# A two-block network on one core: five layer norms run in two halves of 256 tokens, and attention's prologue and branch phase are put in another order

## The reference

```
for l in range(DEPTH):          # DEPTH = 2
    x = layer_norm(alpha * x + 0.5 * swiglu_ffn(x, ffn1_wi[l], ffn1_wo[l]), ln_g[l, 0], ln_b[l, 0])
    mix = even_mixer(x, ...) if l % 2 == 0 else odd_mixer(x, ...)
    x = layer_norm(alpha * x + mix, ln_g[l, 1], ln_b[l, 1])
    x = layer_norm(alpha * x + 0.5 * swiglu_ffn(x, ffn2_wi[l], ffn2_wo[l]), ln_g[l, 2], ln_b[l, 2])
```

```
h = rms_norm(x, g_pre_mix[l]);  proj = h @ w_in[l]
gates = sigmoid(gate_pre.reshape(B, S, 3, D) + b_gate[l])
merged = gates[:, :, 0] * (o_a @ w_br_a[l]) + gates[:, :, 1] * (o_b @ w_br_b[l]) + gates[:, :, 2] * (o_m @ w_br_m[l])
x = x + rms_norm(merged @ w_out[l], g_post_mix[l])
```

## Time and profile before

| | |
|---|---|
| runs of the kernel before, us | 3979.09, 3987.4, 3988.2 (median 3987.4) |
| profiled execution, its own time | 3980.04 us |
| its span | 3978.3 us, mean TensorE clock 0.956 |
| TensorE busy | 3690.6 us, 93% |
| VectorE, ScalarE, GpSimd busy | 1725.9, 1354.3, 606.2 us |

### The profile page before, as it was taken

How to read it: one execution, slowest core, us unless ns; L and a number is a source line. 1 busy time by engine, 2 the same in 40 slices (tenths; PEclk the granted TensorE clock), 3 DMA queues, 4 the chain that set the end, 5 groups by cost and what they waited for, 6 DMA issues and landing times. The chain is left out here.

```text
span 3978.3 us, 44285 instructions
## 1 busy us (share of the span) xinstructions
PE 3690.6 (93%) x17510; PEld 2955.4 (74%) x17510; DVE 1725.9 (43%) x1970; ACT 1354.3 (34%) x1723; POOL 606.2 (15%) x473
## 2 busy tenths in 40 slices
PE   8999987999899989887899989998999898998998
PEld 6887764788688868565688867776888786877886
DVE  2224563322422244753422254555664444547642
ACT  3223432322322233322322242344443323445432
POOL 2102002211311030131311041003110210012110
PEclk9999998999999999877899999999999999999999
DMA  3222211222222222000122233222222233222222
GB/s 138 95 90 95 85 43 43 94 95 87 83 95 98 88 92 85 29 1 13 63 97 96 92 116 111 96 69 95 95 95 91 103 114 104 82 101 85 95 89 80
DMA packets 62080, 339.98 MB, mean 85 GB/s; under 512 B 7024, under 2 KB 11520, under 8 KB 32768
## 3 DMA queue, kind: packets, MB, share of 16 engines
q1 hardware_dynamic: 61952, 338.19, 23.9%
HBM read 331.87 MB, written 6.29 MB: 85 GB/s over the span
## 5 line engine op out<-in xcount | busy, mean ns | idle before, releaser
L355 PE MATMUL bank<-x_hi,w_hi 128*128 128x512 f32 x3488 | 1391.9, 399 | 158.9 <-POOL x_lo L429 77.4
L356 PE MATMUL bank<-x_lo,w_hi 128*128 128x512 f32 x3488 | 1376.5, 395 | 0.0
L357 PE MATMUL bank<-x_hi,w_lo 128*128 128x512 f32 x3488 | 1374.9, 394 | 0.0
L324 DVE TENSOR_TENSOR w_lo<-raw,w_hi 128x2048 fp32r<-128x2048 f32 (+2 forms) x326 | 689.9, 2117 | 970.0 <-ACT w_hi L319 968.6
L355 PEld LDWEIGHTS bank<-x_hi,w_hi 128*128 128x128 f32 x3488 | 666.9, 191 | 337.2 <-issue 145.4
L319 ACT ACTIVATE w_hi<-raw 128x2048 fp32r<-128x2048 f32 (+2 forms) x326 | 567.7, 1742 | 761.6 <-PE bank L357 750.5
L357 PEld LDWEIGHTS bank<-x_hi,w_lo 128*128 128x128 f32 x3488 | 666.2, 191 | 141.4
L356 PEld LDWEIGHTS bank<-x_lo,w_hi 128*128 128x128 f32 x3488 | 666.8, 191 | 137.1 <-issue 1.0
L355 PE MATMUL bank<-f_g_hi,w_hi 128*128 128x512 f32 x704 | 275.5, 391 | 0.0
L357 PE MATMUL bank<-f_g_hi,w_lo 128*128 128x512 f32 x704 | 273.9, 389 | 0.0
L356 PE MATMUL bank<-f_g_lo,w_hi 128*128 128x512 f32 x704 | 273.9, 389 | 0.0
(11 more groups left out here) (402 smaller groups left out, 3425.7 us busy)
## 6 DMA issues: line engine op xcount, KB each, us to landing
raw<-in_weights SPq DMA_DIRECT2D x222, 1024.0 KB, 4.8
raw<-in_weights SPq DMA_DIRECT2D x96, 704.0 KB, 4.0
raw<-in_weights SPq DMA_DIRECT2D x8, 768.0 KB, 4.2
x_kept<-X SPq DMA_DIRECT2D x2, 2048.0 KB, 11.8
X<-x_kept SPq DMA_DIRECT2D x2, 2048.0 KB, 9.6
work<-in_rpb SPq DMA_DIRECT2D x12, 256.0 KB, 5.1
stats<-in_rpb SPq DMA_DIRECT2D x12, 256.0 KB, 5.3
X<-in_x SPq DMA_DIRECT2D x8, 256.0 KB, 6.3
```

The costliest lines, as they stand in the source:

```text
L324: dve.tensor_tensor(w_lo[:, s, 0:size], raw[:, s, 0:size], w_hi[:, s, 0:size].bitcast(F32), ALU.subtract).then_inc(lo_ready.sem, 1)
L355: pe.matmul(out, w_hi[:, s, w], hi(k), start=first and n == 0, stop=False)
L356: pe.matmul(out, w_hi[:, s, w], lo(k), start=False, stop=False)
L357: mm = pe.matmul(out, w_lo[:, s, w], hi(k), start=False, stop=last and n == len(kts) - 1)
```

## The change

Of the six layer norms five (all but the last before attention) are split by tokens. At the end of a stage `last_tile` makes the last product for tokens 0 to 255 first, then for tokens 256 to 511 in two parts with the first half's sums between them; the second half's sums are made in the next stage. At its start `lead_vector`, `lead_scalar`, `lead_pool` go through the eight tiles of the first half and then through those of the second, with the split of the second weight chunk (`split`) in between, and `lead_tensor` takes both first chunks: chunk 0 and 1 for the first half, then chunk 0 and 1 for the second, so that a slot is freed only in the second half. The split of chunk 2 is placed behind this on ScalarE and VectorE. The blocks of the two stages are joined: the engines don't meet between them. The first stage of all, which has no norm, runs in halves too. In attention, `merge` makes its three products from PSUM one behind the other, GpSimd adds the first two, VectorE adds the third in `join(n - 1)`, behind `merge(n)`; TensorE waits for the products alone. ScalarE splits weights ahead of `round_(n)`. In the prologue the first bias goes ahead of the weights' rest, their rounding behind value tile 1 and not 4, and the second part of the first scores behind tile 6 and not 4. The core of the diff:

```diff
+        def lead_vector(dve, split):
...
+            for t in range(2):
+                for k in range(KT + 1):
+                    if k == 0:
+                        if t == 0:
+                            half_variance(dve, norm[0], 0)
+                        dve.wait_ge(half_rstd[norm[0].p].sem, half_rstd[norm[0].p].at(2 * t + 2))
+                    if k < KT:
+                        scale(t, k)
+                    if k == 0:
+                        half_mean(dve, norm[0], t)
+                    if k:
+                        shift(t, k - 1)
+                    if t == 0 and k == 2:
+                        centre_half(dve, norm[0], 1)
+                    if t == 0 and k == 5:
+                        half_variance(dve, norm[0], 1)
+                if t == 0:
+                    split()
...
+        def lead_scalar(act, split):
+            if norm[0] is not None:
+                half_square(act, norm[0], 0)
+                half_scale(act, norm[0], 0)
+            for t in range(2):
+                for k in range(KT):
+                    x, q = X[:, k, halves[t]], t * KT + k
...
+                        act.wait_ge(lead_shifted.sem, lead_shifted.at(q + 1))
+                        act.activation(x, x, ACT.Identity, bias=col("ln_b", n), scale=col("ln_g", n)).then_inc(x_ready.sem, 1)
+                        act.wait_ge(x_ready.sem, x_ready.at(q + 1))
+                    act.activation(x_hi[:, k, halves[t]], x, ACT.Copy).then_inc(rounded.sem, 1)
+                    if t == 0 and k == (KT - 1 if norm[0] is None else 2):
+                        split()
+                    if t == 0 and norm[0] is not None:
+                        if k == 1:
+                            square_half(act, norm[0], 1)
+                        elif k == 4:
+                            half_square(act, norm[0], 1)
+                        elif k == 6:
+                            half_scale(act, norm[0], 1)
...
+        def lead_tensor(pe, n0):
+            pe.wait_ge(lo_ready.sem, PRIME + n0 + 1)
+            for t in range(2):
+                xt, yt = (lambda k: x_hi[:, k, halves[t]]), (lambda k: x_lo[:, k, halves[t]])
+                for k in range(KT):
+                    pe.wait_ge(split_ready.sem, split_ready.at(t * KT + k + 1))
+                    for v in range(2):
+                        mm = linear(pe, bank[v][:, halves[t]], n0 % 2, (v * KT + k) * P, [k], xt, yt, first=k == 0,
+                                    last=k == KT - 1, group=False)
+                    if t == 0 and k == 1 and norm[0] is not None:
+                        half_sums(pe, norm[0], 1)
+                        half_stats(pe, norm[0], 1)
+                if t == 1:
+                    mm.then_inc(chunk_used.sem, 1)
                 else:
+                    pe.wait_ge(lo_ready.sem, PRIME + n0 + 2)
+                for v in range(2):
+                    mm = linear(pe, bank[2 + v][:, halves[t]], (n0 + 1) % 2, v * KT * P, range(KT), xt, yt, group=False)
+            mm.then_inc(chunk_used.sem, 1)
...
+        def half_sums(pe, nb, t):
+            b = bank[7 - t]
+            if t:
+                pe.wait_ge(half_centred[nb.p].sem, half_centred[nb.p].at(2))
+            else:
+                pe.wait_ge(part_ready.sem, part_ready.at(KT - 2))
+                pe.wait_ge(square_used.sem, square_used.at(KT - 2))
+            pe.matmul(b[:, 0:HS], const["mean_d"], nb.acc[:, halves[t]], start=True, stop=False, skip_group_check=True)
+            pe.matmul(b[:, HS:S], const["mean_d"], nb.accq[:, halves[t]], start=False, stop=False, skip_group_check=True)
...
+        def last_tile(pe, nb, pieces, hi, lo):
+            for n, (c, at, ks) in enumerate(pieces):
+                first, last = n == 0, n == len(pieces) - 1
+                mm = linear(pe, out[0], c % 2, at, ks, part(hi, 0), part(lo, 0), first=first, last=last, group=False)
+                if first:
+                    pe.wait_ge(z_ready.sem, z_ready.at(KT - 1))
+                if not last:
+                    linear(pe, out[1], c % 2, at, ks, part(hi, 1), part(lo, 1), first=first, last=last, group=False)\
+                        .then_inc(chunk_used.sem, 1)
+                    continue
+                mm.then_inc(half_psum[nb.p].sem, 1)
+                half_sums(pe, nb, 0)
+                linear(pe, out[1], c % 2, at, ks[:4], part(hi, 1), part(lo, 1), first=first, last=False, group=False)
+                half_stats(pe, nb, 0)
+                linear(pe, out[1], c % 2, at + 4 * P, ks[4:], part(hi, 1), part(lo, 1), first=False, last=True, group=False)\
+                    .then_inc(chunk_used.sem, 1)
...
+                    sp.wait_ge(lead_shifted.sem, lead_shifted.at(KT))
...
-                    split(0, 0)
-                    lead_scalar(act)
+                    lead_scalar(act, lambda: split(0, 0))
+                    split(0, 1)
                     for j in range(n):
-                        if j:
+                        if j > 1:
                             split(j // 2, j % 2)
...
-                    lead_vector(dve)
+                    lead_vector(dve, lambda: split(0, 0))
+                    split(0, 1)
                     for j in range(n):
-                        split(j // 2, j % 2)
+                        if j > 1:
+                            split(j // 2, j % 2)
                         if j < GATES:
                             causal_conv(j, U, 2 * j, "rg_conv", 4, u_ready)
                         if j == 1:
...
-                            elif n == 4:
+                            elif n == 6:
                                 scores(0, 1)
...
@@ -2672,7 +2882,7 @@
                         for n in range(NT):
                             bank_copy(n)
-                            if n == 4:
+                            if n == 1:
                                 at_chunk(split_hi, act, g0 + 1)
                         exps(0)
                         for c in chunks_ending(-1):
...
                         for n in range(KT):
                             if n + 3 < KT:
                                 open_gates(n + 3)
-                            round_(n)
                             if n % 2:
...
                             gate = G[3 * n:3 * n + 3]
-                            ch.add(dve.tensor_tensor(m, b[0], gate[0], ALU.mult))
-                            ch.add(dve.tensor_tensor(q, b[1], gate[1], ALU.mult))
-                            ch.wait()
-                            ch.add(dve.tensor_tensor(m, m, q, ALU.add))
-                            ch.wait()
-                            ch.add(dve.tensor_tensor(q, b[2], gate[2], ALU.mult))
-                            ch.wait()
-                            dve.tensor_tensor(m, m, q, ALU.add).then_inc(y_ready.sem, 1)
+                            dve.tensor_tensor(m, b[0], gate[0], ALU.mult)
+                            dve.tensor_tensor(q, b[1], gate[1], ALU.mult).then_inc(pair_ready.sem, 1)
+                            dve.tensor_tensor(r, b[2], gate[2], ALU.mult).then_inc(state_ready.sem, 1)
+                        def join(n):
+                            v = n % 2
+                            dve.wait_ge(state_ready.sem, state_ready.at(n + 1))
+                            dve.wait_ge(h_ready.sem, h_ready.at(n + 1))
+                            dve.tensor_tensor(mg[:, v, :], mg[:, v, :], rest[:, v, :], ALU.add).then_inc(y_ready.sem, 1)
...
+                        add_bias(0)
                         at_chunk(split_lo, dve, g0 + 1)
-                        add_bias(0)
                         add_bias(0, 1)
...
+                        for n in range(KT + 1):
+                            if n < KT:
+                                merge(n)
+                            if n:
+                                join(n - 1)
                             if n % 2:
                                 at_chunk(split_lo, dve, b0 + n // 2 + 2)
...
                     def _(pool):
-                        for n in range(KT):
-                            pool.wait_ge(rounded.sem, rounded.at(n + 1))
-                            pool.tensor_tensor(x_lo[:, n, :], mg[:, n % 2, :], x_hi[:, n, :].bitcast(F32),
-                                               ALU.subtract).then_inc(split_ready.sem, 1)
+                        for n in range(KT + 1):
+                            if n < KT:
+                                m = mg[:, n % 2, :]
+                                pool.wait_ge(pair_ready.sem, pair_ready.at(n + 1))
+                                pool.tensor_tensor(m, m, part[:, n % 2, :], ALU.add).then_inc(h_ready.sem, 1)
+                            if n:
+                                pool.wait_ge(rounded.sem, rounded.at(n))
+                                pool.tensor_tensor(x_lo[:, n - 1, :], mg[:, (n - 1) % 2, :], x_hi[:, n - 1, :].bitcast(F32),
+                                                   ALU.subtract).then_inc(split_ready.sem, 1)
```

(13 more changed lines are left out.)

241 lines of the change are left out of this document (162 added, 79 removed).

## The result

The changed kernel took 3996.66 us (median of 12 runs, 3991.78 to 4000.83); the kernel before, timed beside it, 3985.01 us (12 runs, 3972.15 to 3998.6). The ratio is 1.0028, with a 95% interval of 1.0016 to 1.0039: slower, by about as little as this kernel's runs can tell. The forecast was 3979, slightly faster. The time lies in the range (3951 to 4004), the direction was wrong. The 3985.01 is a median of runs that lie up to 26 us apart; the kernel before that was timed beside the experiments has medians of 3979.9 to 3980.2.

The account below looks back on a forecast made before the run. TensorE, busy 93% of the span, was taken as the bound, with only waits and slow stretches to win. Seams +12.2, prologue +11.4, branch phase -20.6 made 3.0 us faster than 3980.0: 3977.0, said as 3979; range 3951 to 4004.

Parts of the forecast that it names:

- A feed-forward seam in halves: Passage between stages around a halved norm: 40.1 us instead of 46.3, a gain of 6.2 us, at two of five seams.
- Into the even mixer: Seam ahead of the even mixer: same gain, less 4.4 us for the convolution's banks and nearly 1 for clock; net +1.
- Behind the mixers: Seams behind the two mixers: GpSimd's sum of squares still holds TensorE; gain 1.9 us each, 3.8 together.
- Low clock: All five seams: 1 us a seam allowed for more time at low clock, 5 us in all.
- The rival in which TensorE stays at 1.2 GHz through the first half: Seams: half matmuls at low clock cost 9.6 us a seam; 4020 at worst, middle case 3998; chance of slower 0.23.
- First stage 0: First stage of all, which has no norm: no gain or loss, 0 us.
- Prologue: Attention's prologue: the 5.3 us wait for the first bias goes, plus 0.4 for clock; twice, +11.4 us.
- Branch phase: Attention's branch phase: VectorE's chain takes 14.2 us a pair for 11.25; 10.3 us lost a layer, -20.6.
- The rival that had it hidden: Branch phase: merges' wait for `x_lo` hidden, pair stays 11.25 us, 3956; chance of faster, by this or larger seam gains, 0.36.

Follow-up runs that it names:

- e1: Changed kernel, but TensorE waits for the rest of the last tile's second weight chunk only when it reaches that chunk; 3980.88 us, ratio 1.0000.
- e4: Kernel before, with only the prologue's new order added; 3965.01 us, ratio 0.9964.
- e3: Kernel of e1, with VectorE making the rest of the even mixer's chunk 2 behind the convolution of chunk 0, as before the change; one run, 3974.41 us.
- e11: Kernel of e10, with the first stage's two first chunks at full width, tiles' rounding ahead of the second chunk's weights; 3944.91 us, ratio 0.9909.
- e2: Changed kernel, with attention's branch phase as it was before the change; 3972.02 us, ratio 0.9979.
- e6: Changed kernel, with the weights' split back behind the rounding and their rest behind the join; merge and join stay apart; one run, 3987.41 us.
- e7: Changed kernel with the edits of e1, e3 and e2 together, the prologue's new order kept; 3949.92 us, ratio 0.9924.
- e9: Changed kernel with all of attention (branch phase and prologue) as before, so the halved norms and joined blocks alone; 3987.31 us, ratio 1.0017.
- e5: Changed kernel, with ScalarE opening the gates of n+3 behind an odd n's weights' split in the branch phase; one run, 3984.76 us.
- e8: Kernel of e7, with the first stage at full width and also chunk 1's split ahead of the tiles' rounding; 3961.25 us, ratio 0.9950.
- e10: Kernel of e7 (old merge), with ScalarE splitting an odd n's weights ahead of rounding n in the branch phase; 3942.35 us, ratio 0.9901.

## Why the prediction was wrong, by its steps

- **A feed-forward seam in halves: +6.2 each.** The chain from the first half's last product on was right to a few tenths. What failed is the step ahead of it: "33 half matmuls of the tile are left, 33 x 0.120 = 4.0 us, in before's terms 3.75" takes for granted that TensorE reaches that product as early as it did. The wait for the second chunk in front of the last tile was not in the sum. It is one line of the diff, and it costs 3.2 us of idling and about 2 at 1.2 GHz: three times, 15.6 us (e1). Without it the seams' term is nearly met against the trace of before (C 5.3, D 8.0 for 6.1); against e4's, which has the same instructions there as before, C and D pay 5.1 each.
- **Into the even mixer:** the loss for the convolution's banks was right (4.3 us idle, 4.4 forecast). That the other order gives back only part was worked out before e3 and holds, 1.9 us.
- **Behind the mixers, 1.9 each:** right in that GpSimd's sums hold TensorE, but the gain isn't there. Behind the even mixer:

```profile
698.60 1.19 PE L611 MATMUL bank<-o_sums,consts 128*128 128x256 f32 x2 [10.07 <-POOL o_sums L701]
...
709.78 0.36 PE L375 MATMUL bank<-x_hi,w_hi 128*128 128x256 f32 x1 [3.93 <-POOL x_lo L501]
```

TensorE idles 10.1 and 3.9 us for 6.2 and 8.8 before: 1.0 less, with doubled matmuls against it. From the first matmul of the output projection to the next stage's second product the two seams took 315.4 and 315.2 us before, 313.7 and 313.2 in e4 with the same instructions, and 313.8 to 315.1 and 313.4 to 313.7 in the kernels with halved norms.
- **Low clock, 1 us a seam:** near. The rival in which TensorE stays at 1.2 GHz through the first half did not come true: in seam 1 matmuls are 0.12 apart right behind the 2.86 us of idling, and it is one stretch of 4.9 us, behind a later wait of 3.4 us, that runs at the lower clock.
- **First stage 0:** it is 1.7 us longer. The 13 ns that the text itself gives for each of 96 matmuls were not put into this line of the sum; with the earlier start that half a tile allows they come to 0.6 net (e11). Another 0.8 is the later start of the whole program.
- **Prologue, +11.4:** the mechanism right, the size too small; 16.1. The two waits of 5.3 us went as said, and the waits behind them stayed (e4); the term that was too small is the 0.4 us for the clock behind the first wait. In the changed kernel F and I gain 3.2 and 2.3 beyond the 5.3 (3.1 and 1.2 in e4); only 0.9 of it, in I, are later waits that were shorter.
- **Branch phase, -20.6:** right, 21.7. Every merge of layer 2 starts 5.2 to 5.6 us after the time given for it (3498.9, 3501.0, 3510.1, 3515.3, 3524.3 and so on), and the phase began 5.6 us later. The rival that had it hidden is dead: its chain has no TensorE in it. The joins took 1.39 us: a partner's 0.68 on top of the operation's own, and not more. The Trainium skill (SBUF — State Buffer, SBUF: two separate sides) has a VectorE operation with two inputs there and a GpSimd one that reads it exclude one another for a whole instruction. The join at 3508.36 starts 0.85 us before GpSimd's sum of the next n ends and takes 1.40; the last one, at 3556.03 with GpSimd idle, takes 0.68. So a join waits about for what is left of the sum, and these rows don't speak against the page.

```profile
3507.92 1.29 POOL L3051 TENSOR_TENSOR work<-work 128x512 f32<-128x512 f32 x1 [0.80 <-DVE work L3004]
3508.36 1.40 DVE L3011 TENSOR_TENSOR work<-work 128x512 f32<-128x512 f32 x1
...
3556.03 0.68 DVE L3011 TENSOR_TENSOR work<-work 128x512 f32<-128x512 f32 x1
```

For an execution like the profiled one the text said 3977.0; the changed kernel's profiled execution took 3996.95 (its span is 3995.2). The 20.0 us between are the wait in front of the last tile (15.6), the even mixer's clock (4.7), the first stage (1.7), the branch phase (1.1) and stretches without an edit (1.8), less the prologue's 4.7, which is 20.2. The missing term alone is more than the change's whole loss in the runs: with it put right the kernel is level with the one before (e1, ratio 1.0000), which a gain of 3 us can't be told from. That the time lies in the range is luck: the range reached so high for a rival, TensorE at 1.2 GHz through the first half, that did not come true.

## What to carry to other kernels

When a stage's last tile is cut up, lay out the time in front of it too: a wait that is drawn ahead of two uses, since it is simpler to write, takes away the cover that the first use gave the second. An instruction's place in an in-order queue is good or bad only together with what stands on the chain through that queue: the weights' split ahead of the rounding costs about 1 us of each pair when a sum is deferred behind the next merge, and gives 2.2 when it isn't. In this kernel, with TensorE busy for 93% of the time, halving a norm pays some 5 us at a feed-forward seam (C, and D as a whole), nothing that can be told behind a mixer, where GpSimd's sums hold it, and little or nothing where what frees weight slots or banks moves behind the second half. And a second trace of unchanged instructions, as e4's here, is worth having before a difference of 5 us is put down to an edit.

## What was not expected of the hardware

The scan stage of the even mixer (no edit in any kernel touches it) has two lengths. From the start of its last 192 projection matmuls to the first of the output projection it took 123.3 to 123.8 us in eight of the traces (before, e2, e3, e4, e6, e7, e9, e11) and 127.4 to 128.2 in five (changed, e1, e5, e8, e10). e2 and e5 run the same instructions up to there and differ. Windows of 20 us (busy us and instructions by engine, then the granted clock, DMA share, GB/s), of e5,

```profile
560.00:580.00 20.00, 18.42 (x36) 8.69 (x35) 5.53 (x12) 8.73 (x17) 2.35 (x5) 0.66 0.00 0
```

and of e2:

```profile
560.00:580.00 20.00, 18.42 (x58) 10.81 (x57) 7.22 (x15) 8.73 (x17) 2.36 (x5) 0.91 0.00 0
```

TensorE is busy for the same 18.42 us in both, at a granted clock of 0.66 in one and 0.91 in the other, and gets 36 matmuls done where the other gets 58. So some 4 us of a difference between two single traces of this kernel, and of B in the table, are the clock's and not an edit's; 4.7 of the changed kernel's 17.0 were of this kind. Its runs show 11.6 us and not 17.0 for another reason: its profiled execution is like its median run (3996.95, 3996.66), and that of the kernel before lies 5.0 us below its own (3980.04, 3985.01). The runs of some kernels lie in two groups some 5 us apart as well (e2: four at 3968.0 to 3968.8, five at 3972.0 to 3975.3; e9: two at 3982.9 and 3983.9, nine at 3986.4 to 3988.9); whether these are the two lengths isn't shown, since one trace of each is kept. What decides between the two lengths stays open.
